# Sample states queried four at a time, their updates spread anew, and the last gate product begun at the end of the recurrence

## What is computed

```python
def gla_recurrence(q, k, v, lg, s0):          # per chunk of C tokens, per head
    bcum = jnp.cumsum(lg, axis=3)
    blast = bcum[:, :, :, -1:]
    q_dec = q * jnp.exp(bcum)
    k_intra = k * jnp.exp(-bcum)
    k_state = k * jnp.exp(blast - bcum)
    att = jnp.where(causal, jnp.einsum('nbhid,nbhjd->nbhij', q_dec, k_intra), 0.0)
    o_intra = jnp.einsum('nbhij,nbhje->nbhie', att, v)
    def step(s, inp):
        qc, kc, vc, dc = inp
        o_inter = jnp.einsum('bhid,bhde->bhie', qc, s)
        s = dc[..., None] * s + jnp.einsum('bhjd,bhje->bhde', kc, vc)
        return s, o_inter
    ...
# then, per head: o * rsqrt(mean(o*o)+eps) * norm_g * silu(z), and the output projection
```

## Time and profile before

| | |
|---|---|
| time, median of 3 runs | 1652.73 us |
| lowest, highest | 1651.33, 1653.35 us |
| span of the profiled execution | 1651.1 us |
| PE busy | 1613.4 us, 98% of the span |
| DVE, ACT, POOL busy | 818.7, 458.2, 375.8 us |
| mean granted clock of PE | 0.990 of full speed |

### The profile page before, as it was taken

One profiled execution on the slowest core, in us unless ns is written; L12 is line 12 of the kernel. 1 busy time (PEld: TensorE's weight loads), 2 busy tenths in 40 slices (PEclk: granted clock), 3 DMA queues, 4 the chain that ended last, 5 costly groups with the idle time before them and its releaser, 6 DMA issues.

```text
span 1651.1 us, 25118 instructions
## 1 busy us (share of the span) xinstructions
PE 1613.4 (98%) x9827; PEld 1501.1 (91%) x9827; DVE 818.7 (50%) x1271; ACT 458.2 (28%) x969; POOL 375.8 (23%) x384
## 2 busy tenths in 40 slices
PE   6999999999999999998999999999999999999996
PEld 5899999999999999998788898888998989979896
DVE  4654449443944475457224562245622356224475
ACT  4321112111211121123325413154040541315423
POOL 3022212211211212211314223133130322314310
PEclk8999999999999999998999999999999999999998
DMA  9512221221122121210202212022120221201312
GB/s 330 193 56 87 62 63 42 84 74 42 55 78 64 57 67 54 77 41 27 64 18 73 84 40 77 13 64 84 53 66 12 64 96 40 77 13 40 110 37 108
DMA packets 137545, 115.03 MB, mean 70 GB/s; under 512 B 6013, under 2 KB 120281, under 8 KB 137442
## 3 DMA queue, kind: packets, MB, share of 16 engines
q1 hardware_dynamic: 135616, 112.87, 22.0%
q10 hardware_dynamic: 1834, 0.74, 0.2%
HBM read 99.05 MB, written 15.00 MB: 69 GB/s over the span
## 4 chain that ended last, share of the span: by engine, by line
PE 94%; DVE 3%; SPq 1%; DMA 1%; ACT 1%; issue 0%; ACTq 0%; DVEq 0%
PE psA L549 40%; PE psB L549 29%; PE psB L1804 8%; PE psA L1804 4%; PE psB L1860 2%; PE psB L1877 2%; PE psX L1842 2%; PE psB L1868 2%; PE psX L1897 1%; DVE a_hi L637 1%; PE psB L1909 1%; PE psX L1720 1%; DMA ada<-in_ada_w 1%; DVE y_rows L1606 0%; PE psB L1910 0%; PE psX L1661 0%
## 5 line engine op out<-in xcount | busy, mean ns | idle before, releaser
L344 POOL TENSOR_TENSOR w_lo<-stage,w_hi 128x1024 fp32r<-128x1024 f32 x100 | 249.7, 2496 | 891.1 <-ACT w_hi L339 891.1
L339 ACT ACTIVATE w_hi<-stage 128x1024 fp32r<-128x1024 f32 x100 | 107.0, 1070 | 433.7 <-PE psB L549 297.6
L549 PE MATMUL psA<-h_hi,w_hi 128*128 128x362 f32 (+1 forms) x864 | 210.9, 349 | 4.1 <-DVE h_lo L453 3.8
L549 PE MATMUL psA<-h_lo,w_hi 128*128 128x362 f32 (+1 forms) x864 | 193.6, 329 | 0.0
L549 PE MATMUL psA<-h_hi,w_lo 128*128 128x362 f32 (+1 forms) x864 | 193.1, 329 | 0.0
L549 PEld LDWEIGHTS psA<-h_hi,w_hi 128*128 128x128 f32 x864 | 151.4, 190 | 27.1 <-issue 21.2
L549 PEld LDWEIGHTS psA<-h_hi,w_lo 128*128 128x128 f32 x864 | 151.5, 190 | 0.0
L549 PEld LDWEIGHTS psA<-h_lo,w_hi 128*128 128x128 f32 x864 | 151.4, 190 | 0.0
L549 PE MATMUL psA<-a_hi,w_hi 128*128 128x362 f32 (+1 forms) x480 | 109.7, 334 | 2.6 <-DVE a_lo L640 1.9
L549 PE MATMUL psB<-h_hi,w_hi 128*128 128x362 f32 (+1 forms) x480 | 109.7, 331 | 0.0
L549 PE MATMUL psB<-h_hi,w_lo 128*128 128x362 f32 (+1 forms) x480 | 107.9, 327 | 0.0
(11 more groups left out here) (345 smaller groups left out, 2790.6 us busy)
## 6 DMA issues: line engine op xcount, KB each, us to landing
stage<-in_gla_w_in SPq DMA_DIRECT2D x40, 512.0 KB, 3.8
stage<-in_pool_w_in SPq DMA_DIRECT2D x32, 512.0 KB, 4.1
ada_stage<-in_ada_w SPq DMA_DIRECT2D x24, 512.0 KB, 3.8
ada<-in_ada_w SPq DMA_DIRECT2D x16, 512.0 KB, 8.4
stage<-in_pool_w_out SPq DMA_DIRECT2D x16, 512.0 KB, 3.4
v<-in_state_gla SPq DMA_DIRECT2D x32, 256.0 KB, 2.6
out_new_gla_sample<-v SPq DMA_DIRECT2D x32, 256.0 KB, 2.1
stage<-in_gla_w_out SPq DMA_DIRECT2D x16, 512.0 KB, 3.7
```

The source lines that it names most:

```text
L339: nc.scalar.activation(slot_hi(plan, j), stage[:, j % 2, :], ACT.Copy).then_inc(lay.hi_done, 1)
L344: nc.gpsimd.tensor_tensor(slot_lo(plan, j), stage[:, j % 2, :], slot_hi(plan, j).bitcast(f32), ALU.subtract).then_inc(lay.lo_done, 1)
L549: last = nc.tensor.matmul(ps[u][:, t, 0:width], weight(w[:, p, :], k), a[:, k, n0:n0 + width], start=(k == 0 and pas == 0), stop=(k == kt ...
```

## The change

Three things are edited in each head's recurrence. `sample_inter` handles four samples in a row, at s = 5 and s = 8. A table `SAMPLES` says at which s which samples are updated: 0 at s = 5, 1 and 2 at s = 6, 3 at s = 7, 4 and 5 at s = 8, 6 and 7 at s = 9. The step `fill(1)` at the head of s = 6 stands between samples 1 and 2 instead, and the first two steps of Z3 stand ahead of samples 6 and 7 at s = 9. The rest of Z3 is also made by `fill`, with `mean_square(8)` after two more steps, as before. Each start state has a load semaphore of its own, and SP stores follow the table one s later. In `after` the names stand some lines lower: L1897 is L1906, L1909 and L1910 are L1918 and L1919, L1919 is L1928, L1924 is L1933, L1932 is L1941, L549 is L551, L1507 is L1511.

```diff
--- before.py
+++ after.py
@@ -65,6 +65,8 @@
             ("O01", 1, "01"), ("O23", 1, "01"), ("O45", 1, "01"), ("O67", 1, "01")]
 
 FILL_START, FILL_STEP = 7, 2
+
+SAMPLES = {5: (0,), 6: (1, 2), 7: (3,), 8: (4, 5), 9: (6, 7)}
 
 MINIS = 11
 HIST = 384
@@ -291,7 +293,7 @@
         kT_done, ksT_ready, upd_done, S_ready = sem("kT_done"), sem("ksT_ready"), sem("upd_done"), sem("S_ready")
         smp_arg, smp_exp, smp_ready = sem("smp_arg"), sem("smp_exp"), sem("smp_ready")
         smp_att, smp_attr, smp_kT, ksm_ready = sem("smp_att"), sem("smp_attr"), sem("smp_kT"), sem("ksm_ready")
-        s0_loaded = [sem(f"s0_loaded{i}") for i in range(4)]
+        s0_loaded = [sem(f"s0_loaded{i}") for i in range(NB)]
         s0_stored = [sem(f"s0_stored{i}") for i in range(4)]
         s0_ready, smp_upd = sem("s0_ready"), sem("smp_upd")
         S_stored = sem("S_stored")
@@ -801,7 +803,7 @@
 
                     wait_apart(sp, upd_done, g * NSUP + b + 1)
                     sp.dma_start(v[:, b, :], state_gla[0, b, ds(g, 1), :, :].rearrange("a p n -> p (a n)"))\
-                        .then_inc(s0_loaded[b % 4], 16)
+                        .then_inc(s0_loaded[b], 16)
 
                 def store_state(b):
 
@@ -851,8 +853,10 @@
                         wait_apart(sp, S_ready, (g + 1) * NSUP)
                         sp.dma_start(new_gla_prompt[0, 0, ds(g, 1), :, :].rearrange("a p n -> p (a n)"), S[:])\
                             .then_inc(S_stored, 16)
-                    if s >= 2:
-                        store_state(s - 2)
+                    for b in SAMPLES.get(s - 1, ()):
+                        store_state(b)
+                for b in SAMPLES[NSUP + 1]:
+                    store_state(b)
                 for j in range(GP.slot["O45"], GP.slots):
                     load(j)
 
@@ -1553,8 +1557,9 @@
                 qd_args(1)
                 scale_qk(1)
                 for s in range(NSUP + 2):
-                    if s >= 2:
-                        ks_rows(s - 2)
+                    now = SAMPLES.get(s, ())
+                    if now:
+                        ks_rows(now[0])
                     if s + 1 < NSUP:
                         att_out(s + 1)
                     if s + 2 < NSUP:
@@ -1564,8 +1569,10 @@
                         state(s)
                     if s + 1 < NSUP:
                         scale_qs(s + 1)
-                    if s >= 2:
-                        sample_state(s - 2)
+                    for b in now:
+                        if b != now[0]:
+                            ks_rows(b)
+                        sample_state(b)
 
                 dve.wait_ge(s0_ready, (g + 1) * NB)
                 dve.wait_ge(o_evac, (g + 1) * NSUP)
@@ -1872,8 +1879,10 @@
                 def update(s):
 
                     pe.wait_ge(ksT_ready, g * NSUP + s + 1)
-                    if s >= 3:
-                        pe.wait_ge(s0_ready, g * NB + s - 2)
+                    if s - 1 in SAMPLES:
+                        pe.wait_ge(s0_ready, g * NB + SAMPLES[s - 1][-1] + 1)
+                    elif s:
+                        pe.wait_ge(S_ready, g * NSUP + s)
                     nc.tensor.matmul(ps[1][:, 2, :], ksT[:, s % 2, :], v[:, s, :], start=True,
                                      stop=True).then_inc(upd_done, 1)
 
@@ -1889,8 +1898,8 @@
 
                 def sample_inter(b0):
 
-                    for b in (b0, b0 + 1):
-                        pe.wait_ge(s0_loaded[b % 4], g * 32 + (b // 4) * 16 + 16)
+                    for b in range(b0, b0 + 4):
+                        pe.wait_ge(s0_loaded[b], g * 16 + 16)
                         first = b < 4
                         rows = slice(CG * (b % 4), CG * (b % 4) + CG)
                         c = CG * b + (TS if first else 0)
@@ -1899,11 +1908,11 @@
                     if b == NB - 1:
                         last.then_inc(smp_rows_done, 1)
 
-                def sample_update(b):
+                def sample_update(b, s):
 
                     pe.wait_ge(ksm_ready, g * NB + b + 1)
-                    if b + 2 < NSUP:
-                        pe.wait_ge(S_ready, g * NSUP + b + 3)
+                    if s < NSUP and b == SAMPLES[s][0]:
+                        pe.wait_ge(S_ready, g * NSUP + s + 1)
                     else:
                         pe.wait_ge(s0_ready, g * NB + b)
                     nc.tensor.matmul(ps[1][:, 2, :], ksm[:, 0, :], v_s[:], start=True, stop=False)
@@ -1946,7 +1955,7 @@
                 key_rows(0)
                 fill(FILL_START - 5)
                 for s in range(NSUP + 2):
-                    if s <= NSUP:
+                    if s <= NSUP and s != 6:
                         fill(1)
                     if s + 1 < NSUP:
                         scores(s + 1)
@@ -1958,23 +1967,20 @@
                     if 1 <= s <= NSUP:
                         pe.wait_ge(att_ready, g * NSUP + min(s + 2, NSUP))
                         mean_square(s - 1)
-                    if s in (2, 4, 6, 8):
-                        sample_inter(s - 2)
+                    if s in (5, 8):
+                        sample_inter(0 if s == 5 else 4)
                     if s == NSUP + 1:
                         sample_out()
-                    if s >= 2:
-                        sample_update(s - 2)
+                    for b in SAMPLES.get(s, ()):
+                        if s == NSUP + 1 or (s == 6 and b == 2):
+                            fill(1)
+                        sample_update(b, s)
                 pe.sem_inc(L1.unit_done, 1)
 
-                u = GP.unit["Z3"]
-                set_ready(pe, L1, GP, g, u)
-                slot_ready(pe, L1, GP, g, "Z3")
-                for k in range(KD):
-                    last = product_step(GP.slot["Z3"] % 2, GP.set[u], k, KD, w8, h_hi, h_lo)
-                    if k == 1:
-                        pe.wait_ge(smp_o_evac, g + 1)
-                        mean_square(NSUP)
-                last.then_inc(L1.unit_done, 1)
+                fill(2)
+                pe.wait_ge(smp_o_evac, g + 1)
+                mean_square(NSUP)
+                fill(4 * KD - filled[0])
 
                 u = GP.unit["NRM"]
                 set_ready(pe, L1, GP, g, u)
```

## The result

| | before | after |
|---|---|---|
| time, median of 4 runs each on one chip | 1652.06 us | 1662.03 us |
| lowest, highest | 1651.33, 1653.35 us | 1661.71, 1665.01 us |
| ratio, 95% interval | | 1.0059 [1.0045, 1.0073] |
| span of the profiled execution | 1651.1 us | 1659.8 us |
| mean granted clock of PE | 0.990 | 0.986 |

A forecast was written before the change was run, and what follows sets the result against it. PE, 94% of the chain and never idle in the recurrence or Z3, was the bound. Loop -0.14 and tail +1.23 gave +1.09 us a head, times four +4.4 on 1651.1, plus 1.6 for the median: 1657.1 us, plus or minus 2.3.

The forecast's parts named there:

- Part 1: Recurrence: two sample_inter calls fewer a head, a call of four costing 1.06 us like a pair; -2.12 us a head.
- Rival (c): Query matmuls: only two column groups run at once, +0.86 us for each of two calls, 1664 us; chance 0.05.
- Part 2: Updates 4 and 5 back to back at s = 8: PE waits for DVE, +1.58, about 1.60 us a head.
- (d): Tail: POOL's job begins later or holds longer, DVE's delay 2.7 us instead of 1.2, 1663 us; chance 0.08.
- Part 3: Recurrence: shorter iterations, state loads and stores stay hidden at no cost; failing, at most 0.5 us at five places.
- Part 4: Tail after NRM: fewer Z3 steps cover DVE and ACT, so O01's fourth step waits for low(3); +1.2 us a head.
- Rival (a): Tail absorbs the delay, O01 does not wait, only the loop's -0.14 a head remains; 1652.2 us, chance 0.14.
- the rule quoted in the prediction: Tail: DVE and GpSimd exclude each other on one port pair for a whole instruction; delay 1.2 us, if shared 2.7.

The follow-up runs named there:

- e1: The changed kernel with sample_out moved from s = 9 to between the updates of samples 4 and 5; ratio to before 0.9995.
- the tail's edit: DVE makes gate_product(2) before the reciprocals; ratio to before 1.0023 on the changed kernel, 1.0000 on before itself.
- e0_after: The changed kernel run once more with no edit; 1663.59 us, ratio to before 1.0068.
- e2_tail: The changed kernel with gate_product(2) made on DVE before the reciprocals, nothing else; ratio to before 1.0023.
- e5_pairs: The changed kernel with queries in four calls of two, at s = 4, 5, 7 and 8; ratio to before 1.0104.
- e4: The kernel before with sample_out moved from s = 9 to s = 8, so updates 6 and 7 stand back to back; ratio to before 1.0052.
- e7: The changed kernel with only sample_out's eight narrow products moved between the updates of samples 4 and 5; ratio to before 1.0003.
- e9: The changed kernel with sample_out's eight narrow products between updates 4 and 5, and gate_product(2) before the reciprocals; ratio to before 0.9975.
- e8: The changed kernel with sample_out between updates 4 and 5 and gate_product(2) early, then updates 6 and 7 back to back among wide products; ratio to before 1.0001.

## Why the prediction was right in sign and wrong in size

- **Part 1** held. L1906 x8 takes 1.06 us and the next L1918 starts 1347.45 - 1346.45 = 1.00 behind it (said 0.98). Undone, it costs 2.11 (said 2.12). Rival (c), only two groups at once, is out.
- **Part 2 is the step that failed**, in what it leaves out. The wait itself is as priced: 2.16 us between the two L1918 against 1.82 + 0.3, idle 1.42 to 1.43 against some 1.6, undisturbed loop 74.70 against 74.59. But "Nothing lies between: +1.58" prices the wait by its length alone. It takes PE's speed behind the wait for that of before. The traces show that behind it PE may run at 0.50 for 3.4 or 6.8 us, about 1.5 or 2.95 us lost, in two heads of four in both profiles of this kernel. That is +4.5 on the span, as much again as the whole forecast. The clock column is 1.00 in the earlier trace rows, where PE was never idle (74.73 of 74.73), so no row of the heads could show what a first idle stretch does, and the sum needed an upper bound for it. The warning stood elsewhere in the same trace: at 751.5 us, among one-column matmuls, the clock is 0.50 with PE busy (windows above). The wait was being put among narrow products too. No rival had it either: (d) gives nearly the measured time, 1663, but by a DVE delay of 2.7 that did not happen.
- **Part 3** held. PE's idle time in the undisturbed loop is the one wait (74.70 less 73.28 is 1.42), and without that wait e1's window is busy to 73.18 of 73.18.
- **Part 4** held in its sum and not in its place. DVE, POOL and ACT came as worked out (gate products 2.92 against 2.9, `gate_in(3)` 1.40 behind Z3's end against 1.4), and the path got 1.21 longer, said 1.23. But nearly all of it is ahead of O01's **first** step, released by ACT's `gate_in(3)`, not by `low(3)` ahead of the fourth. O01 writes the PSUM tile psA that Z3 has filled, and `gate_in(3)` is what empties it. I had followed only the data of the fourth step, and not who frees the tile that the first one writes. The rows of `before` stood on that edge already: `gate_in(3)` ends at 936.90 + 1.20 = 938.10, and O01's first step starts at 938.25. Both waits hang on the same 1.2 us, so the sum came out in spite of the wrong place; had `low(3)` caught up meanwhile, 1.11 would have been paid all the same. Rival (a) is out.
- On the shared port of DVE and POOL, the trace has this row (first head of `after`):

```profile
926.87 2.41 POOL L346 TENSOR_TENSOR w_lo<-stage,w_hi 128x1024 fp32r<-128x1024 f32 x1 [2.10 <-DVE ksm L1505]
```

POOL ends at 929.28 and the gate products at 928.77 + 2.92 = 931.69, 2.41 us later, as it was 2.42 in `before`. They meet only the last 0.5 us of POOL's job and take 2.92 us instead of 4.41; with that, the delay of `gate_in(3)` is 1.2 and not 2.7. Of the rule quoted in the prediction from the Trainium skill (SBUF — State Buffer, section SBUF: two separate sides), the trace agrees: the delay is the one that the exclusive lock gives.

- **The numbers.** The forecast's own range, plus or minus 2.3, took in only the uncertainty of waits that it knew. With the clock's fall in two heads of four, 1657.1 + 4.5 = 1661.6, against 1662.0 measured. That the two meet so closely is in part luck: the forecast starts from 1652.7 for `before`, where the comparison has 1652.1, and the 4.5 is that of one profiled execution.

## What to carry to other kernels

A wait put into a stretch where PE never idled is priced by its length and by what the clock may do behind it, so look at the neighbours: among wide products 1.42 us cost its length here (four heads of one profile), among narrow ones up to three times as much. Fill such a gap with independent work that the program has anyway (here `sample_out`, already there and needed a few steps later) before giving up the regrouping that caused it; this turned +0.6% into nothing (0.9995), and with the tail's edit into -0.3% (0.9967). And when filler is moved ahead of the end of a recurrence, follow the side engines' chain to the next product's operands and also to whoever empties its PSUM tile.

## What the runs showed of the hardware that was not expected

- PE's granted clock fell from 1.00 (2.4 GHz) to 0.50 (1.2 GHz) behind a wait of 1.42 us that stood between narrow products, in 9 of the 16 heads profiled in `after`, e0_after, e2_tail and e5_pairs, in 1 of 4 in e4, and in none of the heads with 0.61 us there (e7, e9), nor with 1.42 us among wide products (e8). In the two heads of `after` the half clock lasted 6.8 and 3.4 us and cost 2.95 and 1.53 us. Which head it hits changes from execution to execution. Whether it widens the scatter of the times is not shown: they range over 9.8 us in e0_after, but over 7.0 in `before` (1651.0 to 1658.0 on one chip) and 6.9 in e1_apart. The Trainium skill (TensorE: Matmul & The Clock Gate, section HAM oscillation — how this bites in real kernels) tells of a clock halved behind waits of 3 to 5 us between bursts; here 1.42 us among narrow products were enough, and the measurement decides.
- In `before`, 54 one-column matmuls with no idle time between them took the granted clock from 1.00 to 0.50 about 5 us after their start (window 751.50:752.50).
- The rows with half clock show DMA traffic beside them (0.41 at 1351) and also none (0.00 at 1353): the half clock went on without transfers.
- Four fp32 queries in four column groups take 1.06 us, two in two groups 1.05 (after, e5_pairs).
